# Paced modulation chunks, small vectors on two queues, the last gate's sums and the last second map moved

## The reference, cut to what matters

```python
mod = silu(c) @ w_mod + b_mod            # 6 x 1024: sh1 sc1 g1 sh2 sc2 g2; the same for c_ctx
u = rmsnorm(tokens) * (1 + sc1) + sh1    # context and latent
x_rnn, g_rnn, x_pool, m_rnn, m_pool = split(u @ w_in)
# RG-LRU in both directions over context, then latent; pooling mixer over the latent grid
merged = sigmoid(m_rnn) * (y_rnn @ w_rnn_proj) + sigmoid(m_pool) * (y_pool @ w_pool_proj)
x = x + g1 * rmsnorm(merged @ w_out)
v = rmsnorm(x) * (1 + sc2) + sh2
# top 4 of 32 experts, softmax weights comb
for e in range(32):
    z = v @ w1[e] + b1[e]                # 1024 -> 2048, clamped SwiGLU -> 1024
    out += comb[:, e] * (act @ w2[e] + b2[e])
x = x + g2 * rmsnorm(out)                # output, 256 x 1024
```

## Time and profile before

| | us |
|---|---|
| median of three runs | 1302.9 (1300.26 to 1303.01) |
| profiled execution | 1308.87 |
| its span | 1307.0 |
| TensorE busy | 1260.6 |
| TensorE waits for a DMA before its first instruction | 10.9 |
| TensorE waits for w_in at 223 us | 7.23 |
| TensorE waits for expert weights, 13 times | 9.7 |
| mean granted TensorE clock | 0.991 of full |

### The profile page before, as it was taken

The page is one execution under the profiler, slowest core; times in us unless marked ns, Lnnn a source line. Parts: engine busy times, 40 slices in busy tenths (PEclk is TensorE's granted clock), DMA queues, the critical chain, the costliest instruction groups (busy, mean ns, idle before and its releaser), DMA issues.

```text
span 1307.0 us, 13909 instructions
## 1 busy us (share of the span) xinstructions
PE 1260.6 (96%) x5686; PEld 548.3 (42%) x5686; DVE 350.3 (27%) x633; ACT 216.9 (17%) x366; POOL 26.3 (2%) x72
## 2 busy tenths in 40 slices
PE   5999998999999999999999999999999999999996
PEld 3445687878443333333333333333333333333331
...
DMA  9733569587388999999999999999999999999994
GB/s 360 257 122 97 187 237 391 183 321 278 141 333 363 430 426 428 428 427 429 426 429 426 428 427 427 417 427 428 427 427 427 428 427 428 427 427 427 428 427 195
DMA packets 74159, 476.03 MB, mean 364 GB/s; under 512 B 7056, under 2 KB 38992, under 8 KB 47472
## 3 DMA queue, kind: packets, MB, share of 16 engines
...
## 4 chain that ended last, share of the span: by engine, by line
PE 75%; DMA 16%; ACT 4%; DVE 3%; issue 1%; ACTq 0%; DVEq 0%; SPq 0%
PE bank L829 28%; PE bank L840 15%; DMA arena<-in_exp_w 13%; PE bank L708 10%; PE bank L804 4%; PE bank L851 4%; PE bank L599 2%; PE bank L629 2%; PE bank L576 2%; DMA arena<-in_w_in 2%; PE bank L813 2%; PE bank L894 1%; PE bank L646 1%; ACT arena L998 1%; ACT arena L992 1%
## 5 line engine op out<-in xcount | busy, mean ns | idle before, releaser
L829 PE MATMUL bank<-arena,temps 128*64 128x512 f32 x2112 | 463.6, 594 | 9.7 <-DMA arena<-in_exp_w 9.7
L829 PEld LDWEIGHTS bank<-arena,temps 128*64 128x64 f32 x2112 | 147.7, 137 | 322.0 <-issue 300.1
L840 PE MATMUL bank<-arena,temps 128*64 128x512 f32 x1056 | 233.9, 595 | 0.6 <-DVE temps L1534 0.6
L1527 DVE TENSOR_SCALAR temps<-bank 128x512 f32<-128x512 f32 x33 | 22.8, 691 | 667.2 <-PE bank L829 667.2
L840 PEld LDWEIGHTS bank<-arena,temps 128*64 128x64 f32 x1056 | 72.7, 137 | 138.2 <-issue 132.1
L708 PE MATMUL bank<-arena 128*128 128x256 f32 x512 | 114.4, 386 | 7.2 <-DMA arena<-in_w_in 7.2
L708 PEld LDWEIGHTS bank<-arena 128*128 128x128 f32 x512 | 99.3, 194 | 23.4 <-issue 9.5
L1105 ACT ACTIVATE temps<-temps 128x512 f32<-128x512 f32 x33 | 20.8, 630 | 507.7 <-DVE temps L1527 507.7
L851 PE MATMUL bank<-temps,hot 64*128 64x512 f32 x264 | 65.6, 615 | 0.8 <-ACT temps L1113 0.8
L804 PE MATMUL bank<-vtokb,hot 128*64 128x512 f32 x256 | 63.7, 619 | 0.0
L646 PE MATMUL bank<-arena 128*128 128x512 f32 x128 | 56.3, 593 | 0.3 <-ACT arena L993 0.3
(11 more groups left out here) (256 smaller groups left out, 838.0 us busy)
## 6 DMA issues: line engine op xcount, KB each, us to landing
...
arena<-in_w_in SPq DMA_DIRECT2D x20, 1024.0 KB, 6.7
arena<-in_w_mod POOLq DMA_DIRECT2D x16, 1024.0 KB, 7.5
arena<-in_w_mod SPq DMA_DIRECT2D x8, 1024.0 KB, 15.3
arena<-in_w_pool_proj SPq DMA_DIRECT2D x4, 1024.0 KB, 5.1
arena<-in_w_rnn_proj SPq DMA_DIRECT2D x4, 1024.0 KB, 7.4
arena<-in_w_out SPq DMA_DIRECT2D x4, 1024.0 KB, 10.4
...
```

Source lines behind the costliest of these rows:

```text
L829: last = mm(psum[4 + q][h * SLOTS:(h + 1) * SLOTS, :], xg[:, k // 4, k % 4, :], w1_at[s][:, r, o:o + HALF], start=False, stop=(k == KT - 1))
L840: last = mm(psum[6][h * SLOTS:(h + 1) * SLOTS, :], actT[:, c, r, :], w2_at[s][:, r, h * HALF:(h + 1) * HALF], start=(c == 0 and r == 0), s ...
```

## The change

- *Front.* ScalarE issues every other small vector, SP the rest behind the token tiles. load_mod has eight DMAs of 512 KB a group, with a semaphore for each 256 rows, and mod_columns waits for those. The square root and its scaling run for two tiles at a time. VectorE reads the turning jobs xt 0 to 3, ScalarE xt 4 to 7.
- *w_mod chunks 7 to 15* on GpSimd wait for the jobs gg 0, gg 1, and so on, one job a chunk, beside the waits that they had. The seven bias and norm rows are issued by GpSimd behind them; SP no longer issues them.
- *g2.* Six row sums instead of eight. VectorE multiplies the partial sums for g2 with the norm row and adds the bias row on partition 0 (g2_part); SP's loads of w_out wait for that too. TensorE sums it with the matrix of ones in item 0 (sum_g2), and ScalarE takes it out (g2_ready). In item 0 the gather now comes before bias_rows, which waits for g2_ready.
- *w_out.* The first six k steps of wo(0, 0) wait for three parts of merged, the last two for the fourth.
- *Last item.* The second map runs in two column halves (second_map_halves) into two banks, each with its own eviction; the last scatter goes by the same halves.

```diff
@@ -74,14 +74,14 @@
 
 
     plan = [("vec", 0, "V")]
-    plan += [("xt", n, "VA"[n % 2]) for n in range(2 * 4)]
+    plan += [("xt", n, "VA"[n // 4]) for n in range(2 * 4)]
     plan += [("xr", j, "A") for j in range(4)]
     for s in range(2 * HEADS):
         plan += [("lru", s, None), ("xr", s + 4, "A") if s < 4 else ("xp", s - 4, "A")]
     for kind in ("gg", "mr", "mp"):
         plan += [(kind, c, "A") for c in range(4)]
     plan += [("pw", g, "A") for g in range(4)]
-    plan += [("rs", n, "A") for n in range(8)]
+    plan += [("rs", n, "A") for n in range(6)]
     plan += [("pp", c, "V") for c in range(4)]
     plan += [("rp", c, "V") for c in range(4)]
...
@@ -398,16 +399,17 @@
 
             def load_mod(g):
 
-                for n in range(2 * g, 2 * g + 2):
-                    r = slice(n % 2 * HALF, (n % 2 + 1) * HALF)
+                for n in range(4):
+                    r = slice(n * 256, (n + 1) * 256)
                     for w in range(2):
                         o = w * D + g * HALF
-                        sp.dma_start(modw[2 * n + w], w_mod[r, o:o + HALF].rearrange("(k p) n -> p k n", p=P)).then_inc(
-                            mod_landed[n], 16)
+                        sp.dma_start(modw[2 * (2 * g + n // 2) + w][:, n % 2 * 2:n % 2 * 2 + 2, :],
+                                     w_mod[r, o:o + HALF].rearrange("(k p) n -> p k n", p=P)).then_inc(mod_landed[4 * g + n], 16)
 
             for t in range(4):
                 src = I["ctx" if t < 2 else "x"][0, t % 2 * P:(t % 2 + 1) * P, :]
                 sp.dma_start(xin[:, t, :], src).then_inc(tokens_landed[t], 16)
+            load_vectors(sp, (ROWS1 + ROWS2)[1::2])
             for n, parts in enumerate(chunks):
                 if n < 2:
...
@@ -422,12 +424,6 @@
                     else:
                         dst = dst.rearrange("p (k n) -> p k n", k=src.shape[1])
                     sp.dma_start(dst, src).then_inc(ring_landed[n % RING], 16)
-                if n == chunk_no["mr", 3]:
-                    sp.wait_ge(lru_done, 2 * HEADS)
-                    for g, c in (("g1", 2), ("sh2", 3), ("sc2", 4), ("g2", 5)):
-                        sp.dma_start(brow[g], xrows(I["b_mod"][0:1, c * D:(c + 1) * D])).then_inc(brow_landed, 16)
-                    for g, name in (("g1", "norm_post_mix"), ("sc2", "norm_pre_ffn"), ("g2", "norm_post_ffn")):
-                        sp.dma_start(nrow[g], xrows(I[name])).then_inc(brow_landed, 16)
                 if n == chunk_no["pp", 2]:
                     sp.wait_ge(job_done, number["mp", 3] + 1)
                     load_expert(0, 0, 0)
@@ -435,7 +431,8 @@
                     sp.wait_ge(job_done, number["pw", 3] + 1)
                     load_expert(0, 0, 1)
                 if n == chunk_no["rp", 0]:
-                    sp.wait_ge(job_done, number["rs", 7] + 1)
+                    sp.wait_ge(job_done, number["rs", 5] + 1)
+                    sp.wait_ge(g2_part, 1)
                     for c in range(4):
                         sp.dma_start(wo_w[c], I["w_out"][0, c * 256:(c + 1) * 256, :].rearrange(
...
@@ -516,9 +513,16 @@
                 k, h, q = n // 2, n % 2, GM_AT[n]
                 if n == GM_EARLY:
                     pool.wait_ge(lru_done, 2 * HEADS)
+                if n >= GM_EARLY:
+                    pool.wait_ge(job_done, number["gg", 0] + 1 + (n - GM_EARLY))
                 if q in GM_AT[:n]:
                     pool.wait_ge(gm_done, max(m for m in range(n) if GM_AT[m] == q) + 1)
                 pool.dma_start(slot(GM_SLOTS[q]), w_mod[k * P:(k + 1) * P, (h + 1) * CW:(h + 2) * CW]).then_inc(gm_landed[q], 16)
+
+            for g_row, c in (("g1", 2), ("sh2", 3), ("sc2", 4), ("g2", 5)):
+                pool.dma_start(brow[g_row], xrows(I["b_mod"][0:1, c * D:(c + 1) * D])).then_inc(brow_landed, 16)
+            for g_row, name in (("g1", "norm_post_mix"), ("sc2", "norm_pre_ffn"), ("g2", "norm_post_ffn")):
+                pool.dma_start(nrow[g_row], xrows(I[name])).then_inc(brow_landed, 16)
 
...
@@ -606,7 +610,7 @@
 
                 for k in range(KT):
                     n = 2 * g + k // 4
-                    pe.wait_ge(mod_landed[n], 32)
+                    pe.wait_ge(mod_landed[4 * g + k // 2], 32)
...
@@ -724,10 +728,12 @@
                 elif kind == "vt":
                     t, q = n // 2, n % 2
                     if n == 0:
-                        pe.wait_ge(merged_ready, 4)
+                        pe.wait_ge(merged_ready, 3)
                         pe.wait_ge(gates_read, 2 * HEADS)
                         pe.wait_ge(wo_landed, 16 * 4)
-                        wo(0, 0)
+                        wo(0, 0, 0, 6)
+                        pe.wait_ge(merged_ready, 4)
+                        wo(0, 0, 6, KT)
                         wo(0, 1)
...
@@ -841,6 +847,32 @@
                                       w2_at[s][:, r, h * HALF:(h + 1) * HALF], start=(c == 0 and r == 0), stop=(c == 1 and r == 3))
                     last.then_inc(w_used, 1)
 
+            def second_map_halves(i):
+
+                for q in range(2):
+                    for c in range(2):
+                        s = slot_of(i, 4 + c)
+                        if q == 0:
+                            pe.wait_ge(expert_landed[s], landed_at(i, 4 + c))
+                        for r in range(4):
+                            for h in range(2):
+                                o = h * HALF + q * 256
+                                last = mm(psum[6 + q][h * SLOTS:(h + 1) * SLOTS, 0:256], actT[:, c, r, :], w2_at[s][:, r, o:o + 256],
+                                          start=(c == 0 and r == 0), stop=(c == 1 and r == 3))
+                    last.then_inc(y_half, 1)
+
+            def scatter_halves(n):
+
+                pe.wait_ge(gt_ready, n + 1)
+                for t in range(TT):
+                    for q in range(2):
+                        pe.wait_ge(y_ready, n + (1 + q))
+                        for h in range(2):
+                            r = slice(h * SLOTS, (h + 1) * SLOTS)
+                            last = mm(psum[2 * t + h][:, q * 256:(q + 1) * 256], gt[r, t * P:(t + 1) * P], yS[r, q * 256:(q + 1) * 256],
+                                      start=False, stop=False, skip_group_check=True)
+                    last.then_inc(scatter_done, 1)
+
             def scatter(n):
 
...
@@ -861,8 +893,15 @@
                               start=True, stop=True)
                 last.then_inc(table_done, 1)
 
+            def sum_g2():
+
+                pe.wait_ge(g2_part, 1)
+                for h in range(2):
+                    mm(psum[2 + h][:, :], ones[:, :], g2row[:, h * HALF:(h + 1) * HALF], start=True, stop=True).then_inc(g2_summed, 1)
+
             def bias_rows():
 
+                pe.wait_ge(g2_ready, 2)
                 pe.wait_ge(ct_read, 1)
                 pe.wait_ge(cnt_read, 1)
...
@@ -880,13 +919,14 @@
                 first_map(i, first)
                 if first:
                     turn_table()
-                    bias_rows()
+                    sum_g2()
+                    bank_read(6)
                 else:
                     scatter(i - 1)
-                if first:
-                    bank_read(6)
                 if not last:
                     gather(i + 1)
+                if first:
+                    bias_rows()
                 pe.wait_ge(act_ready, i + 1)
                 if first:
...
@@ -900,7 +940,10 @@
                     turned = nc.tensor.transpose(psum[5][:, t * P:(t + 1) * P], selw[:, t, :], ident[:, :])
                 turned.then_inc(spread_done, 1)
                 pe.wait_ge(actT_ready, i + 1)
-                second_map(i)
+                if last:
+                    second_map_halves(i)
+                else:
+                    second_map(i)
...
@@ -913,13 +956,13 @@
             with pe.Fori(FIXED, last_item) as i:
                 item(i)
             item(last_item, last=True)
-            scatter(last_item)
+            scatter_halves(last_item)
 
 
...
-            load_vectors(act, ROWS1 + ROWS2)
+            load_vectors(act, (ROWS1 + ROWS2)[0::2])
             chain = [0]
 
...
@@ -939,23 +982,23 @@
                 act.wait_ge(tokens_landed[t], 16)
                 a.activation(temps[:, 2048:3072], xin[:, t, :], ACT.Square, accum_out=stat[:, t:t + 1]).then_inc(ssq_ready, 1)
                 act.wait_ge(ssq_ready, t + 1)
-            act.wait_ge(rstd_var, 1)
-            a.activation(stat[:, 8:12], stat[:, 4:8], ACT.Sqrt).then_inc(rstd_root, 1)
+                if t % 2:
+                    act.wait_ge(rstd_var, t // 2 + 1)
+                    a.activation(stat[:, 7 + t:9 + t], stat[:, 3 + t:5 + t], ACT.Sqrt).then_inc(rstd_root, 1)
             act.wait_ge(read_dve, 1)
             a.activation(small[:, 0:16], vecT[:, 0:16], ACT.Tanh, scale=0.5).then_inc(silu_th, 1)
 
-            for t in range(4):
-                b = job_of("xt", 2 * t + 1)
```

(56 more changed lines are left out.)

14 lines of the change are left out of this document (5 added, 9 removed).

## The result

The changed kernel takes **1293.86 us** (median of 6 runs, 1293.55 to 1295.61), the kernel before 1302.45 (6 runs, 1299.07 to 1303.01): ratio 0.9943, 95% interval 0.9931 to 0.9955. That is 8.6 us less, where the forecast said 16.2 less; the time lies 0.9 us above the range of the prediction (1282.5 to 1293).

What follows compares the result with a forecast made beforehand. TensorE's waits were taken to bound the stages before the expert stage, the weight stream the expert stage. Six terms summed to -16.2 us: 1292.7 for the profiled execution, 1286.7 as median, range 1282.5 to 1293.

Steps and rivals of the forecast that it cites:

- b: Mixing products: pacing w_mod chunks and moving rows off SP's queue removes the w_in wait and slow clock, -10.3 us.
- rival 2: Wait at the mp products only halved or moved by DMA crowding; 4 us remain, 1293 us; chance 0.11.
- e: Item 0 reordered, with g2's sums and gather before the bias rows: second map sooner at held clock, -1.2 us.
- c: Row sums: six instead of eight, -1.7 us.
- Rival 1: Clock falls in item 0 after the reorder, costing +2.7 us against the forecast, 1289.4 us; chance 0.25.
- a: Front: small vectors on two queues and roots by pairs let TensorE start near 9.4 us, -1.0 us.
- d: First w_out products start on three of four merged parts, removing the wait for VectorE, -1.55 us.
- f: Tail: last second map and scatter in column halves, -0.45 us.
- The lever: Expert stream starts at item 0's second map: time won before counts fully, between it and the last item not at all.
- Rivals 3 and 4: Transfers bound throughout, only the tail's gain counts, 1302.5 us (0.04); GpSimd's late broadcasts hold SP ahead of w_out, 1307 (0.05).

Runs made afterwards that it cites:

- after_unpaced: Changed kernel without the pacing of GpSimd's w_mod chunks 7 to 15, the seven rows staying on GpSimd's queue: 1297.15 us, ratio 0.9957.
- after_rows_sp: Changed kernel with the seven bias and norm rows back on SP's queue, pacing kept: 1295.74 us, ratio 0.9957.
- experiment 4: On one chip, the changed kernel once more (1296.14 us, ratio 0.9948) and with both pacing and row move undone (1300.33 us, ratio 0.9979).
- front_only: Kernel before with only the new front (vectors on two queues, roots by pairs, w_mod in quarters): 1300.58 us, ratio 0.9997.

## Why the prediction was wrong

The step that failed is the first line of the working: "the median of the runs shown is 1302.9, 6.0 less, and I move the sum over to it unchanged". With it the term of b was mis-sized: -10.3 by the profiled execution, -2 to -4 by the medians. The 6.0 us were no constant. They lay in two terms of the sum, and the change can't win them again where they are not lost.

- **b, forecast -10.3, measured -2 to -4.** The mechanism is right: no wait, full clock, the products right behind each other, mp 0 landed at 208.1 (forecast 208), g2's part ready at 254.7 (forecast by 255). But 7.23 and 3.1 are the stall and the low clock of an execution as slow as one in twelve. Other executions wait 2.8, 3.1 and, with b undone in the changed kernel, 3.7 us, with 0 to 2.9 of low clock; the medians with and without b are 4.2 us apart in the changed kernel, 2.0 in the one before. My bounds were -10.8 and -6, both from this one stall; rival 2 had thought of "4 us remain" after the change, not that there might be only 4 us before.
- **e, forecast -1.2, measured -1.1 against the first profile and +1.8 against an execution whose clock holds.** The 9.12 us are what was forecast for the held clock (8.8 from the sums on, which begin 0.2 behind the table; measured 8.95). The comparison was made with a fallen clock again: 10.20 in the first profile, 7.33 at the full clock. Seen from there, part e is the move of c's 1.7 us to item 0, and c and e cancel. Rival 1 was half right: in neither profile of the changed kernel did the clock fall, but in those of two near variants it did (S-T 9.82 and 9.50), and there the second map itself ran longer than its 7.09, first in after_unpaced, then in after_rows_sp:

```profile
387.69 7.79 PE L844 MATMUL bank<-arena,temps 128*64 128x512 f32 x32
386.86 8.15 PE L847 MATMUL bank<-arena,temps 128*64 128x512 f32 x32
```

  Together that is 1.4 us each, half of rival 1's price of 2.7.
- **a, forecast -1.0, measured 0 to -1**: the vectors landed at 10.4, not 9.4.
- **c (-1.7) and d (-1.55)** came as forecast: 12 records in 5.31 us, and no idle ahead of w_out's products, whose start follows the job before without a gap.
- **f, forecast -0.45, measured -0.6 to -0.7** in executions where clock and chunk are in time.
- **The lever held.** L-S is 887.05 after, 887.35 before. It is no constant either: the second profile of the changed kernel has 888.19 with the second map at full length, 1.1 us that I can't place. Rivals 3 and 4 are out: SP's new wait let go at once, and w_out was there.
- **The range was added up wrongly.** The bounds given for the terms sum to -18.6 and -6.9, not to -20 and -8, and the upper end was then set at 1293 by rival 2. Carried over to the median as they stand, the bounds reach up to 1296, and the measured 1293.86 lies inside. That would have been luck, since b lies outside its own bounds (-10.8 and -6).

Worked again with the usual execution (the third one of the kernel before against the profile after, spans 1298.8 and 1291.7): 3.1 of wait, 1.7, 1.55 and 0.6 that I could not place make the -7.0 from M to W (the 1.55 ends at W); +0.3 in the norm stage, +0.1 in item 0 (-1.65 of low clock and +1.8 of work), +0.1, and -0.7 in the tail: -7.1. The medians moved by 8.6 on the first chip and by 5.5 on the one of experiment 4 (ratios 0.9943 and 0.9948), and 7.1 lies between. Rare large losses move no median; they show in the slow end: of the 58 runs of before, nine are more than 3 us above the median of their chip, and of 66 runs of the eight versions that keep one half of b or both, one is above its own median by as much (1303.11 us, with the rows on SP's queue). Without b the count is uneven, two of 12 in front_only and none of 12 in after_without_b.

What the prediction could have seen: all three runs shown lay 5.9 to 8.6 below the profiled execution, and its clock was 0.991 on a core that stands at full for nearly all of the span. Two losses in it, 10.3 at w_in and 2.9 in item 0, were of the kind that depends on the moment (a transfer just late, a clock that falls), and I see no other place in it where 6 us could be. Taken off there, the sum is some -8 to -10 and the forecast 1293 to 1295.

What stays open: why mp 0 lands after 19.8 us in one execution of the kernel before and after 27.8 in another, when GpSimd's chunks go out at the same distance from it and land in 7 to 10 us in both. One thing goes with it: in the five executions without any of b, in the order of the landing of mp 0 (19.8, 19.9, 22.2, 24.3, 27.8), SP's own issue of mp 2 took 2.3, 2.5, 3.5, 6.2 and 9.3 us; in the changed kernel it took 0.37. Which of the two is the cause isn't shown. No edit here bears on that, and only three profiles of the kernel before show it. It is open, too, in which share of executions item 0's clock falls, with the old order or the new.
